# Stick-breaking scores on both halves of the rows, and two more gate panels between the heads

## The reference, cut to what matters

```
u = causal_depthwise_conv(u, conv_w, conv_b)          # 512 channels, 31 taps
u = silu(layernorm(u)) ; y_conv = u @ w_conv_out
z = einsum("bqhd,bkhd->bhqk", qf, kf)                  # scores, q scaled
log_keep  = where(s < t, log_sigmoid(-z), 0)
log_after = cumsum(log_keep, reverse=True) - log_keep
a = where(s < t, exp(log_sigmoid(z) + log_after), 0)   # stick-breaking weights
o = einsum("bhqk,bkhd->bqhd", a, vf) ; y_att = o @ w_att_out
merged = sigmoid(g_conv) * y_conv + sigmoid(g_att) * y_att
```

## Time and profile before

| what | value |
|---|---|
| median of 3 runs | 1380.03 us (1379.72 to 1380.03) |
| profiled execution, its own time | 1376.84 us |
| span of that profile, first to last instruction | 1375.0 us |
| PE busy | 1351.4 us, 98% |
| PE weight loads busy | 1175.8 us, 86% |
| DVE, ACT, POOL busy | 987.4, 715.3, 173.8 us |
| mean granted TensorE clock | 0.997 |

### The profile page before, as it was taken

One profiled execution on the slowest core, in us unless ns is written; L12 is line 12 of the kernel. 1 busy time (PEld: TensorE's weight loads), 2 busy tenths in 40 slices (PEclk: granted clock), 3 DMA queues, 4 the chain that ended last, 5 costly groups with the idle time before them and its releaser, 6 DMA issues.

```text
span 1375.0 us, 19803 instructions
## 1 busy us (share of the span) xinstructions
PE 1351.4 (98%) x7788; PEld 1175.8 (86%) x7788; DVE 987.4 (72%) x1390; ACT 715.3 (52%) x1170; POOL 173.8 (13%) x155
## 2 busy tenths in 40 slices
PE   9999999999999999999999999999999999999997
PEld 7888888788769999998887778888778999998885
DVE  6899899678587878878326774667687888776332
ACT  4466776553475555573224544556465555564221
POOL 3379343200010000004000010110000000000000
PEclk9999999999999999999999999999999999999998
DMA  9423112455701332324522144431220323333221
GB/s 346 166 82 103 47 47 77 141 182 186 303 16 62 97 119 92 121 95 155 178 96 92 62 131 131 117 99 32 92 77 32 123 92 109 107 108 108 92 92 62
DMA packets 44542, 153.62 MB, mean 112 GB/s; under 512 B 5857, under 2 KB 6113, under 8 KB 44322
## 3 DMA queue, kind: packets, MB, share of 16 engines
q1 hardware_dynamic: 42882, 149.70, 32.7%
q0 software_dynamic: 1568, 2.65, 0.9%
HBM read 143.39 MB, written 2.10 MB: 106 GB/s over the span
## 4 chain that ended last, share of the span: by engine, by line
PE 89%; DVE 7%; ACT 3%; issue 1%; POOL 0%; DVEq 0%; ACTq 0%; POOLq 0%
PE ps L1719 27%; PE ps L1721 27%; PE ps L1720 27%; PE ps L1869 1%; DVE t_buf L1079 1%; PE ps L1807 1%; PE ps L2116 1%; DVE w_lo L1045 1%; PE ps L1761 1%; PE ps L1772 1%; PE ps L1773 1%; PE ps L1777 1%; DVE h_lo L1071 1%; ACT w_hi L559 0%; PE ps L2097 0%
## 5 line engine op out<-in xcount | busy, mean ns | idle before, releaser
L1719 PE MATMUL ps<-h_hi,w_hi 128*128 128x256 f32 (+1 forms) x1120 | 374.1, 334 | 3.0 <-ACT sq L787 1.1
L1721 PE MATMUL ps<-h_hi,w_lo 128*128 128x256 f32 (+1 forms) x1120 | 371.6, 332 | 0.0
L1720 PE MATMUL ps<-h_lo,w_hi 128*128 128x256 f32 (+1 forms) x1120 | 371.5, 332 | 0.0
L1045 DVE TENSOR_TENSOR w_lo<-raw,w_hi 128x1024 fp32r<-128x1024 f32 x141 | 183.9, 1308 | 114.7 <-ACT w_hi L559 113.6
L1719 PEld LDWEIGHTS ps<-h_hi,w_hi 128*128 128x128 f32 x1120 | 212.9, 190 | 26.8 <-issue 3.5
L1721 PEld LDWEIGHTS ps<-h_hi,w_lo 128*128 128x128 f32 x1120 | 212.8, 190 | 20.4
L1720 PEld LDWEIGHTS ps<-h_lo,w_hi 128*128 128x128 f32 x1120 | 212.9, 190 | 19.5 <-issue 0.5
L559 ACT ACTIVATE w_hi<-raw 128x1024 fp32r<-128x1024 f32 x141 | 148.1, 1055 | 145.5 <-PE ps L1721 73.4
L1035 DVE TENSOR_TENSOR w_lo<-quads,w_hi 128x1024 fp32r<-128x1024 f32 (+1 forms) x152 | 164.9, 1086 | 72.7 <-ACT w_hi L559 72.7
L559 ACT ACTIVATE w_hi<-quads 128x1024 fp32r<-128x1024 f32 (+1 forms) x152 | 144.3, 949 | 78.2 <-PE ps L1721 76.6
L1719 PE MATMUL ps<-act_hi,w_hi 128*128 128x512 f32 x352 | 137.0, 389 | 0.0
(11 more groups left out here) (308 smaller groups left out, 2270.0 us busy)
## 6 DMA issues: line engine op xcount, KB each, us to landing
quads<-in_ffn_in SPq DMA_DIRECT2D x76, 512.0 KB, 4.5
raw<-in_ffn_out SPq DMA_DIRECT2D x44, 512.0 KB, 3.7
raw<-in_ada SPq DMA_DIRECT2D x32, 512.0 KB, 4.3
raw<-in_qk SPq DMA_DIRECT2D x25, 512.0 KB, 3.7
ada<-in_ada SPq DMA_DIRECT2D x16, 512.0 KB, 7.7
raw<-in_gates SPq DMA_DIRECT2D x16, 512.0 KB, 3.7
raw<-in_v SPq DMA_DIRECT2D x12, 512.0 KB, 3.8
raw<-in_ffn_in SPq DMA_DIRECT2D x12, 512.0 KB, 4.2
```

The lines of the kernel that those rows point to most:

```text
L1045: nc.vector.tensor_tensor(w_lo[SLOT[p]][:], raw[q % RAW][:], w_hi[SLOT[p]][:].bitcast(f32), ALU.subtract).then_inc(raw_used, 1)
L1719: nc.tensor.matmul(out, w[0], v[0], start=start, stop=False, **kw)
L1720: nc.tensor.matmul(out, w[0], v[1], start=False, stop=False, **kw)
L1721: return nc.tensor.matmul(out, w[1], v[0], start=False, stop=stop, **kw)
```

## The change

Three things change.

**Scores.** A copy of key blocks 1 to 3 and of the queries from column 128 on (`k_twin`, `q_twin`, both parts) is put on the other half of the partitions by two DMAs a head, issued by POOL in the midst of its sums (`twin`, at the sums in `TWIN_AT`). Key block 0 is multiplied on the head's own rows and the others on the other rows. The three matmuls of blocks 1 and 0 are issued in turn, then those of blocks 2 and 3. `z_done` now counts 2 a head.

**Gate panels.** The loop over heads now takes gate panels 1 to 10 (`PANELS_AT`): heads 2 and 5 take two, the second one behind `scores(n + 2)`. Behind each extra panel DVE does 4 more taps. After the loop are gates 11 to 15, and the mean stands behind the first of them. The 6 last products are issued by ACT behind `head_out(7)` in one go. Gate panels 8 and 9 are kept in `acc` and `gate_a9`, copied plainly and given their sigmoid at i == 14, where `gate_c` gets its own.

**Lambda load.** `lam4` makes room for `gate_a9` and is loaded at the start of the feed-forward part, where it had been loaded after the ninth panel.

```diff
+PANELS_AT = [(1,), (2,), (3, 4), (5,), (6,), (7, 8), (9,), (10,)]
+TWIN_AT = {9: (0, 1), 30: (2,), 33: (3,), 36: (4,), 39: (5,), 42: (6,), 45: (7,)}
...
+        qk_both = place("qk_both", [P, 2, 8, SEQ], f32r, at=A0)
+        qk_hi, qk_lo = qk_both[:, 0, :, :], qk_both[:, 1, :, :]
+        q_twin = place("q_twin", [P, 2, SEQ - P], f32r, at=A0 + 63 * K)
+        k_twin = place("k_twin", [P, 2, SEQ - P], f32r, at=t_at + 5 * K)
...
-        GATE_BANK = [7] * 9 + [0, 1, 2, 7, 0, 1, 2]
+        GATE_BANK = [7] * 11 + [0, 1, 2, 7, 0]
...
         @block.sync
                 if (name, i) == ("ffn_in1", 1):
                     sp.wait_ge(mg_c, KT)
                     sp.dma_start(x[:], t["x"]).then_inc(x_again, 16)
+                    sp.wait_ge(mg_a, KT)
+                    sp.dma_start(lam4[:], t["lam"].partition_broadcast(P)).then_inc(lam_in, 16)
...
         @block.gpsimd
+            def twin(h):
+                own, other = slice(HD * (h % 2), HD * (h % 2) + HD), slice(HD - HD * (h % 2), P - HD * (h % 2))
+                pool.wait_ge(lo_of["qk1"], 2 * (h // 2) + 2)
+                if h >= 2:
+                    pool.wait_ge(z_done, 2 * (h - 1))
+                nc.gpsimd.dma_start(k_twin[other, :, :].bitcast(f32), qk_both[own, :, 4 + h // 2, P:SEQ].bitcast(f32))\
+                    .then_inc(twin_in[h % 2], 16)
+                nc.gpsimd.dma_start(q_twin[other, :, :].bitcast(f32), qk_both[own, :, h // 2, P:SEQ].bitcast(f32))\
+                    .then_inc(twin_in[h % 2], 16)
+
             for n, (c, j) in enumerate(SUM_ORDER):
+                for h in TWIN_AT.get(n, ()):
+                    twin(h)
                 pool.wait_ge(tap_prod, n + 3)
...
         @block.scalar
                 if h + 2 < HEADS:
                     soft(h + 2)
+                for i in PANELS_AT[h][1:]:
+                    prepare("gates", i)
+                    gate_tile(i)
             head_out(HEADS - 1, qk_hi, pv_done, o_hi)
-            products(4)
-            gate_tile(KT)
-            for i in range(KT + 1, 2 * KT):
+            products(len(SUM_ORDER))
+            gate_tile(KT + 2)
+            for i in range(KT + 3, 2 * KT):
                 prepare("gates", i)
-                if i == 9:
-                    products(len(SUM_ORDER))
                 gate_tile(i)
...
                 if i == 14:
+                    for m in range(2):
+                        nc.scalar.activation(gate_a_of(m), gate_a_of(m), ACT.Sigmoid).then_inc(gate_sig, 1)
...
         @block.vector
                 taps(4)
+                for i in PANELS_AT[h][1:]:
+                    feed("gates", i)
+                    taps(4)
...
         @block.tensor
+                other = rows_of(n + 1)
+                pe.wait_ge(twin_in[n % 2], 32 * (n // 2 + 1))
+                hi_lo = (0, 0), (0, 1), (1, 0)
+                for kb, term in ((1, 0), (0, 0), (1, 1), (0, 1), (1, 2), (0, 2),
+                                 (2, 0), (2, 1), (2, 2), (3, 0), (3, 1), (3, 2)):
                     c, at = KEY_BANK[kb]
                     w = SEQ - P * kb
+                    a, b = hi_lo[term]
+                    if kb == 0:
+                        key = qk_both[rows, a, 4 + n // 2, 0:P]
+                        query = qk_both[rows, b, n // 2, :]
+                    else:
+                        key = k_twin[other, a, P * (kb - 1):P * kb]
+                        query = q_twin[other, b, P * (kb - 1):SEQ - P]
+                    ins = nc.tensor.matmul(ps[:, 3 * (n % 2) + c, at:at + w], key, query, start=False, stop=term == 2,
+                                           **free)
+                    if term == 2 and kb in (0, 3):
+                        ins.then_inc(z_done, 1)
...
-                gate(n + 1)
+                gate(PANELS_AT[n][0])
                 if n + 2 < HEADS:
                     scores(n + 2)
+                for i in PANELS_AT[n][1:]:
+                    gate(i)
             stick_out(HEADS - 1)
-            for i in range(KT + 1, 2 * KT):
+            for i in range(KT + 3, 2 * KT):
                 gate(i)
                 if i == 11:
                     pe.wait_ge(tap, len(TAP_ORDER))
```

More of the change, by code:

```diff
@@ L186, in build @@
         gate_a = place("gate_a", [P, KT, SEQ], f32, at=A0 + 48 * K)
+        gate_a9 = place("gate_a9", [P, SEQ], f32, at=c_at + 4 * K)
         cv_hi = place("cv_hi", [P, CT, SEQ], f32r, at=A0 + 32 * K)
@@ L287, in build @@
         both_in, row_in = sem("both_in"), sem("row_in")
+        twin_in = [sem(f"twin_in{i}") for i in range(2)]
         dn_sq, dn_ms, dn_eps, dn_rstd, dn_o, dn_norm, dn_hi, dn_ready = (
@@ L324, in build, with gate_a_of @@
         Q_BANK = [(0, 0), (0, 128), (1, 0), (2, 0)]
+        def gate_a_of(m):
+            return acc[:] if m == 0 else gate_a9[:] if m == 1 else gate_a[:, m, :]
         def prob_of(n):
@@ L658, in soft @@
                 zb = 3 * (h % 2)
-                act.wait_ge(z_done, h + 1)
+                act.wait_ge(z_done, 2 * (h + 1))
                 if h:
@@ L683, in gate_tile @@
                     nc.scalar.activation(gate_c[:, i, :], ps[:, GATE_BANK[i], :], ACT.Copy).then_inc(gate_out, 1)
+                elif i < KT + 2:
+                    nc.scalar.activation(gate_a_of(i - KT), ps[:, GATE_BANK[i], :], ACT.Copy).then_inc(gate_out, 1)
                 else:
-                    nc.scalar.activation(gate_a[:, i - KT, :], ps[:, GATE_BANK[i], :], ACT.Sigmoid)\
+                    nc.scalar.activation(gate_a_of(i - KT), ps[:, GATE_BANK[i], :], ACT.Sigmoid)\
                         .then_inc(gate_out, 1)
@@ L1255, in _ @@
                     softplus(h + 1)
-                feed("gates", h + 1)
+                feed("gates", PANELS_AT[h][0])
                 dve.wait_ge(a_hi_ready, h + 1)
@@ L1284, in _ @@
                                                 ALU.subtract).then_inc(cv_ready, 1)
-            dve.wait_ge(gate_sig, 2)
+            dve.wait_ge(gate_sig, 4)
             def merge_lo(m):
@@ L1850, in scores @@
                                      stop=False, **free)
-                for kb in range(NB):
+                other = rows_of(n + 1)
[3 more added lines that the diff above has]
+                                 (2, 0), (2, 1), (2, 2), (3, 0), (3, 1), (3, 2)):
                     c, at = KEY_BANK[kb]
                     w = SEQ - P * kb
-                    keys, queries = slice(P * kb, P * (kb + 1)), slice(P * kb, SEQ)
-                    ins = mul(ps[:, 3 * (n % 2) + c, at:at + w],
-                              (qk_hi[rows, 4 + n // 2, keys], qk_lo[rows, 4 + n // 2, keys]),
-                              (qk_hi[rows, n // 2, queries], qk_lo[rows, n // 2, queries]), False, True, **free)
-                ins.then_inc(z_done, 1)
+                    a, b = hi_lo[term]
[9 more added lines that the diff above has]
+                        ins.then_inc(z_done, 1)
             def suffix_sums(n):
@@ L1891, in gate @@
             def gate(i):
-                if 0 < i <= KT:
+                if 0 < i <= KT + 2:
                     pe.wait_ge(gate_out, i)
@@ L1895, in gate @@
                     pe.wait_ge(lo_of["qk1"], 8)
-                elif i == KT + 1:
+                elif i == KT + 3:
                     pe.wait_ge(a_exp, 3 * HEADS)
-                elif i >= 12:
+                elif i >= 14:
                     pe.wait_ge(gate_out, i - 3)
```

13 lines of the change are left out of this document (5 added, 8 removed).

## The result

The changed kernel takes 1390.68 us (median of 4 runs, 1388.46 to 1391.28), the kernel before 1379.88 us on the same chip (4 runs, 1379.35 to 1380.03). The ratio is 1.0087, 95% interval 1.0074 to 1.0100: slower by 10.8 us by the medians and by about 12 by the ratio, where I had forecast 1381.0 and a range up to 1386.2. The profiled execution is the slowest of the four (1391.28 us), and its mean granted clock is the lowest (0.988, against 0.990 and 0.991).

A forecast was written before the change was run, and what follows sets the result against it. TensorE, busy for 98% of the span, was taken to bound the kernel. The terms summed to 5.1 - 8 S, +0.9 us with S = 0.52, added to 1380.03: 1381.0 us, range 1377.0 to 1386.2.

The forecast's parts named there:

- Scores: Scores of each head: of each pair of matmuls only the longer counts, saving 0.52 us a head, 4.2 us in all.
- rival 2: Scores: turning from one half to the other costs 0.10 us, six turns in 8 heads, 4.8 more: 1389.9 us; chance 0.04.
- rival 1: Scores: the halves don't overlap, S = 0, the wait for POOL stays and 5.1 us is lost: 1385.1 us; chance 0.18.
- The copies: 16 DMAs on POOL's queue, 2 a head: POOL loses up to 1.1 us a head; taken as nothing, at worst 1 us.
- DVE in the heads: Loop over heads: of 12.6 us a head DVE works 12.4 in one and 10.5 in the next, so little spare time.
- The extra gate panels: Loop over heads: DVE's added work fits in a panel's 5.47 us; the wait before `stick_out(7)` goes from 1.67 to 0.8.
- The 0.3 us expected before the `merge` panels: Behind the mean: ACT's two more sigmoid tiles at i == 14 make TensorE wait 0.3 us; bounds 0 and 1.
- The mean: Before the mean: TensorE waits about 5.6 us for POOL's six last sums, which take 9.48 us; mean begins 0.6 later.
- rival 3: Gap before the mean: the clock falls while TensorE waits, costing nothing to 3.59 us; at half, 1382.8 us; chance 0.22.
- 5.1 - 8 S: The whole change in us, S being what a head's scores save; with S = 0.52 it is +0.9.

The follow-up runs named there:

- experiment 2: Against the changed kernel, the copies of head 2 issued before sum 33 in place of sum 30: 1384.40 us, ratio 1.0042.
- experiment 3: New scores, gate panels in their old places, all 16 copies issued by SP and none by POOL: 1379.34 us, ratio 1.0013.
- experiment 1: The changed kernel's two parts apart: new scores with old gate places, 1384.37 us; moved gate panels with old scores and no copies, 1385.38 us.
- 7: Two kernels: copies_by_sp with one tap moved out of each head from 4 on, 1378.54 us; then taps dealt out by DVE's slack, 1378.24 us.
- 8: copies_by_sp without the 21 products and sums between heads 0 to 6, left out altogether: 1372.77 us, ratio 0.9959.
- 9: 21 taps of ACT and POOL given to DVE: against copies_by_sp, 1374.63 us; the same on the kernel before, as control, 1379.39 us.
- gates_only: The changed kernel with its moved gate panels, but the old scores and no copies: 1385.38 us, ratio 1.0058.
- mean_kept_warm: The changed kernel with 12 small matmuls between gate 11 and the wait before the mean: 1388.23 us, ratio 1.0072.
- copies_by_sp: New scores, gate panels in their old places, all 16 copies issued by SP among its loads: 1379.34 us, ratio 1.0013.
- scores_only: The changed kernel with its new scores and copies, but gate panels, products and taps in their old places: 1384.37 us, ratio 1.0050.
- copy_two_later: The changed kernel with the copies of head 2 issued before sum 33 in place of sum 30: 1384.40 us, ratio 1.0042.
- scores_grouped: copies_by_sp with three score matmuls of block 1 and then three of block 0, not in turn: 1379.42 us, ratio 1.0012.
- vector_takes_sums: copies_by_sp with the 21 taps that ACT and POOL work on between the heads given to DVE: 1374.63 us, ratio 0.9981.
- products_in_loop: The changed kernel with 4 products a head in place of 3 between the heads: 1397.44 us, ratio 1.0147.

## Why the prediction was wrong

**Scores: right, and larger.** The step took 0.52 us a head on the ground that of each pair only the longer counts; it is 0.68. Turning from half to half costs nothing to be seen (rival 2), and the halves overlap (rival 1). The step missed that the next block starts beside the last matmul of the pairs. What the Trainium skill states in "TensorEngine Tiling (Array Packing)", Key Properties, that tiles load and multiply independently, agrees with the rows: two matmuls start together at 153.60.

**The copies: the step that failed first.** I counted POOL's issues, up to 1.1 us a head (1.2 in the rows), and found POOL with time to spare, "so I take nothing, at worst 1 us". I looked at who waits for POOL and not at who shares something with it. With the issue before sum 30 and the three sums behind it, a subtraction of DVE took 5.55 us. TensorE waited 3.3, and the clock cost 3.4 more. Moving that one copy gave 5.2 us in the stretch and 6 in the time (experiment 2). It is shown for this issue with sums right behind it. Where the sums came later, in the other heads, no subtraction was held. The four issues before sum 9 went the way that I had named, through the sums, the products and ACT, and I had let two panels of lead cover them. They cover the panels but not `v_lo`, which came 2.1 us late by it: 1.06 us of wait by themselves (experiment 2), none when SP issues the copies (3). The landing was no cost: the copies landed 3.1 us after their issue in the median, and no `scores` waited for one.

**DVE in the heads: the second.** I wrote that the loop "has spare time on ACT, little on DVE", 12.40 of 12.60 us in one head, and then let the scores take 0.5 us off TensorE's share with no term for it. Where TensorE needs 11.9 us a head and DVE 12.4 (experiment 3), DVE is the bound. It shows most where TensorE has no scores to do, before `stick_out(6)`: 3.7 us and 1.6 of clock. That a debt adds up there over the heads is my reading of the rows. It is there without a moved panel (experiment 1), is shifted by moving taps (7), and goes with the sums (8, 9). The price for the eight heads, 5.4 us, is all that the scores save.

**The extra gate panels.** I had said that their DVE work fits, and that the wait before `stick_out(7)` would shrink from 1.67 to 0.8. In gates_only, the clean case, it is 1.80, and a new one of 0.80 stands before `stick_out(6)`: the forecast failed, by 1.8 us in all. The 0.78 of the changed kernel matches it by luck, as two waits come ahead of it there. The 0.3 us expected before the `merge` panels did not come: no wait stands there.

**The mean: right.** A wait for POOL's six last sums was forecast at 5.6 us and measured 4.54, also in gates_only. The sums took 8.46 instead of 9.48 us:

```profile
256.58 8.46 POOL L501 TENSOR_TENSOR conv<-conv,tap_buf 128x512 f32<-128x512 f32 x6 [13.18 <-ACT tap_buf L666]
```

**The clock: rival 3, three times.** I had it at 0.22, for one gap, at 1.8 us as the likely price and 3.59 at most. It came true at each of the three long waits (3.3, 3.7 and 4.5 us) and cost 7.5 us. The Trainium skill ("TensorE: Matmul & The Clock Gate", Part 1) names idleness as what halves the clock, and this trace agrees. I had argued that the work before the gap was dense. That didn't protect it, and the work before the other two was as dense. In mean_kept_warm 2.84 us of small matmuls inside the gap did protect it, and the same mean ran at 3.67 us. What such a wait costs differs between executions: a wait of 3.67 us before `stick_out(6)` had 3.4 us of lower clock with it in the changed kernel and copies_by_sp, and 6.8 in scores_only, copy_two_later and scores_grouped. So a us or two of each stretch is chance.

**The sum.** The change was to be 5.1 - 8 S. Its 0.3 behind the mean lies outside the stretch, so with S measured at 0.68 it gives 4.8 - 5.4 = -0.6 there, and the stretch shows +13.6. Of the difference of 14.2, the wait before `scores(1)` is 3.3, that before `stick_out(6)` 3.7, the clock 7.5, and a suffix sum's wait 0.5: 15.0, with -1.1 for POOL's earlier end, and 0.3 are left over. The subtraction that stands still and DVE as the bound were missing, the four early issues had been priced at nothing, and the clock stood outside the forecast, as a rival that strikes once where it struck three times.

**What stays open.** What DVE's subtraction was held by is not shown: the runs say only that it begins during an issue, that sums follow the issue at once, and that it ends behind the last of them. The issue alone doesn't do it: in the changed kernel an `sb_lo`, also with two operands from SBUF, begins within an issue with no sum behind it for 3.7 us, and takes its usual time. POOL, then DVE:

```profile
173.37 1.04 POOL L490 DMA_DIRECT2D k_twin<-qk_both  x1
174.33 1.49 DVE L1264 TENSOR_TENSOR sb_lo<-sb_e,sb_hi 128x1280 fp32r<-128x1280 f32 x1
```

Why the panels alone wait longer before the last two `stick_out` is open too. With vector_takes_sums the moved panels were not tried; as POOL's sums before the mean are unchanged in it, I would expect them to bring back its wait.

## What to carry to other kernels

When the bounding engine gets less to do, read how busy the next one is in the same stretch: if its idle time is less than what is saved, the saving ends there and shows as a wait in another place, often heads later. A queue with time to spare isn't a free place for a DMA issue: look at what runs beside it on the engine that slows when this one works, and issue where no such work follows. Look, too, at what the queue's own work feeds: an issue can be late for somebody three engines on. Count every new wait of 3 us and more on TensorE 1.3 to 2 times, for the clock behind it (5.6 us cost 1.9 more in products_in_loop, 3.3 cost 3.4 more here).

## What the runs showed of the hardware

- Two matmuls of 64 rows, one on each half, start within 0.01 us of each other and run together; twelve take 1.37 us instead of 2.05. The order in which they are issued, in turns or three and three, makes no difference.
- A subtraction of 128 x 1024 on DVE that began within a DMA issue of POOL took 5.55 to 5.57 us in four profiles with three sums of POOL right behind the issue, and 6.59 with four. It ended 1.1 us after the last sum. A subtraction of 128 x 1280 in the same place, at 182.38 in products_in_loop, took 5.30 instead of 1.49. Two that began within an issue without sums behind it took 1.49, at 174.33 and 203.67 in the changed kernel. Beside sums alone the one of 128 x 1024 took 2.31, beside nothing 1.22. The sums themselves ran faster meanwhile: 3.78 / 3 = 1.26 us each, against a median of 1.74.
- POOL's sums stretch DVE's taps from 0.74 to 1.22 us in the mean, and its subtraction of 128 x 1280 from 1.49 to 2.37. These read two operands from SBUF. The steps that read one of them from PSUM keep their time: `head_lo` takes 0.68 us with the sums and without, and the three parts of a softplus 1.61 us beside sums (at 122.59 in the changed kernel) and 1.61 without (at 156.96 in copies_by_sp). The Trainium skill ("SBUF — State Buffer", SBUF: two separate sides) says that DVE instructions with two SBUF inputs and GpSimd's share a pair of ports under a lock that is held for a whole instruction, and that the loser stands still. The rows agree with that for the instructions with two operands. That one subtraction stood still over three and four sums, not one, is more than it says. The cast to `sb_hi`, with one operand from SBUF, slowed as well, from 0.83 to 1.53 us.
- The clock fell to the lower level behind, or late in, waits of TensorE of 3.3, 3.7 and 4.5 us, and stayed there for 6.8, 3.4 and 6.8 us, although TensorE worked again for all but the first 0.2 us of the second and 1.8 of the third. It did not fall at waits of 1.06, 1.28, 1.87 and 2.31 us.
